# A streaming encoder step on one core: gate products ahead of the position mixing, low parts of the gate weights ahead of the squares, a place of its own for the high part of u

## What is computed

```python
z = h @ w_in + b_in
a = z[..., :2 * D_CONV]
uv = z[..., 2 * D_CONV:2 * D_CONV + 2 * D_GMLP]
gates = jax.nn.sigmoid(z[..., 2 * D_CONV + 2 * D_GMLP:])
a = jax.nn.glu(a, axis=-1)
a = jax.nn.silu(layer_norm(depthwise_causal_conv(a_full, conv_w, conv_b), ln_g, ln_b))
y_a = a @ w_a
uv = jax.nn.gelu(uv)
u, v = uv[..., :D_GMLP], uv[..., D_GMLP:]
v = layer_norm(v, v_ln_g, v_ln_b)
y_b = spatial_gate(u, v, w_s, b_s) @ w_b      # per group of 128 channels: u * (w_s @ v + b_s)
merged = gates[..., :D_MODEL] * y_a + gates[..., D_MODEL:] * y_b
return merged @ w_o, new_hist, v
```

## Time and profile before

| | |
|---|---|
| time before, median of 3 runs | 964.99 us (964.0 to 968.25) |
| span of the profiled execution | 963.2 us |
| TensorE busy | 845.6 us (88%) |
| VectorE busy | 509.0 us (53%) |
| ScalarE busy | 190.9 us (20%) |
| GpSimd busy | 168.8 us (18%) |
| mean granted TensorE clock | 0.940 of full speed |

### The profile page before, as it was taken

One profiled execution on the slowest core, in us unless ns is written; L12 is line 12 of the kernel. 1 busy time (PEld: TensorE's weight loads), 2 busy tenths in 40 slices (PEclk: granted clock), 3 DMA queues, 4 the chain that ended last, 5 costly groups with the idle time before them and its releaser, 6 DMA issues. The chain is left out here.

```text
span 963.2 us, 12133 instructions
## 1 busy us (share of the span) xinstructions
PE 845.6 (88%) x4994; PEld 618.5 (64%) x4994; DVE 509.0 (53%) x753; ACT 190.9 (20%) x284; POOL 168.8 (18%) x156
## 2 busy tenths in 40 slices
PE   2899999999998879979999999917999987979776
PEld 1688886347997879978878644605666655545432
DVE  1328999999999443351365543481333331222236
ACT  3211211111233121741120011201111110101003
POOL 1000000000045454143223000001122221121110
PEclk9899999999998889989999999856999998989899
DMA  9923225011332131365999593242999999999936
GB/s 323 315 64 88 65 67 174 1 44 44 89 88 57 48 88 45 88 219 175 316 314 322 186 381 149 97 193 83 411 404 416 415 418 394 368 406 394 373 110 248
DMA packets 112600, 204.16 MB, mean 212 GB/s; under 512 B 9484, under 2 KB 68212, under 8 KB 104350
## 3 DMA queue, kind: packets, MB, share of 16 engines
q1 hardware_dynamic: 94192, 159.36, 46.5%
q10 hardware_dynamic: 12830, 34.93, 9.6%
q0 software_dynamic: 5520, 9.06, 2.5%
HBM read 199.49 MB, written 14.84 MB: 223 GB/s over the span
## 5 line engine op out<-in xcount | busy, mean ns | idle before, releaser
L858 PE MATMUL PS<-arena 128*64 128x256 f32 (+1 forms) x1056 | 148.7, 411 | 30.2 <-issue 25.7
L1280 DVE SCALAR_TENSOR_TENSOR arena<-arena,VT 128x574 f32<-128x574 f32 x240 | 175.1, 811 | 0.0
L858 PEld LDWEIGHTS PS<-arena 128*64 128x64 f32 (+1 forms) x1056 | 108.8, 156 | 65.4 <-issue 36.9
L1695 POOL TENSOR_TENSOR wL<-arena,wH 128x1024 fp32r<-128x1024 f32 x32 | 83.2, 2621 | 360.8 <-ACT wH L998 360.8
L552 PE MATMUL PS<-arena 128*128 128x272 f32 x512 | 119.1, 396 | 1.6 <-DVE arena L1242 1.6
L552 PEld LDWEIGHTS PS<-arena 128*128 128x128 f32 x512 | 98.3, 192 | 22.1 <-issue 1.6
L619 PE MATMUL PS<-gH,wH 128*128 128x272 f32 x384 | 83.0, 299 | 9.1 <-POOL wL L1695 5.5
L1591 DVE TENSOR_TENSOR arena<-PS,arena 128x256 f32<-128x256 f32 x19 | 8.1, 424 | 140.1 <-ACT arena L1114 140.1
L619 PE MATMUL PS<-gL,wH 128*128 128x272 f32 x384 | 81.9, 296 | 0.0
L619 PE MATMUL PS<-gH,wL 128*128 128x272 f32 x384 | 81.7, 294 | 0.0
L878 PE MATMUL PS<-arena 128*64 128x512 f32 (+1 forms) x264 | 69.1, 597 | 1.4 <-DVE arena L1595 1.4
(11 more groups left out here) (282 smaller groups left out, 996.9 us busy)
## 6 DMA issues: line engine op xcount, KB each, us to landing
arena<-w_gate SPq DMA_DIRECT2D x32, 1024.0 KB, 7.3
arena<-w_up SPq DMA_DIRECT2D x32, 1024.0 KB, 15.4
arena<-w_down ACTq DMA_DIRECT2D x28, 1024.0 KB, 13.9
arena<-w_in SPq DMA_DIRECT2D x40, 512.0 KB, 5.2
arena<-w_ada SPq DMA_DIRECT2D x8, 2048.0 KB, 14.4
vecs<-w_ada SPq DMA_DIRECT2D x4, 2048.0 KB, 9.3
arena<-x_prompt SPq DMA_DIRECT2D x8, 512.0 KB, 8.0
arena<-w_in SPq DMA_DIRECT2D x4, 1024.0 KB, 6.3
```

The costliest lines, as they stand in the source:

```text
L858: last = pe.matmul(PS[h * rows:(h + 1) * rows, 2, n * DE:(n + 1) * DE], hG[:, b, k * SLOTS + h * rows:k * SLOTS + (h + 1) * rows], buf[r / ...
L1280: dve.scalar_tensor_tensor(out=total, in0=src, scalar=tap, in1=total, op0=ALU.mult, op1=ALU.add).then_inc(conv_step, 1)
L1695: pool.tensor_tensor(wL2[q % 2][:, m], WP[q % 2][:, m], wH2[q % 2][:, m], ALU.subtract).then_inc(gw_split, 1)
```

## The change

- TensorE: the order becomes gate 0, histories, gate 1, histories, gate 2, `over_features(6)`, gates 3, 4, 5, then four times two mixes and one gate (gates 6 to 9), gates 10 to 13, `over_features(4)`, gates 14 and 15. The output projection starts when the last but one branch product is merged, and waits for `merged` tile by tile in its first product.
- GpSimd: no gain and bias of v. The low parts of gate unit 2 come ahead of the wait for v, those of units 3, 4 and 5 ahead of the squares.
- VectorE: all of v, in the order of the tiles. The low parts of u (`low_of(0, uT, uL)`) follow the sum of the squares, ahead of the wait for `c_std`.
- ScalarE: the copies of u's high part, four behind the drain of gate 10 and four behind that of gate 12. The root, the first branch unit's high part, the drain of gate 14, swish of tiles 0 to 3, the drain of gate 15, swish of tiles 4 to 7.
- Memory: `yH` and `vecs` share a place behind the arena, `cT32` gets its own, the first buffer of the conditioning weights (`AW[0]`) moves to the place of `gL`, `c16` and `iotaI` lie in the place of u at the start of the program.
- SyncE: the first conditioning weights are loaded when gate 15 is done.

```diff
-        yH, uL, aL = split_parts("yH", O_X, KT, T), split_parts("uL", O_U, KT, T), split_parts("aL", O_C, KT, CONV)
+        yH, uL, aL = split_parts("yH", ARENA, KT, T), split_parts("uL", O_U, KT, T), split_parts("aL", O_C, KT, CONV)
...
-        AW = [vecs[:, 0:KT * BLK].rearrange("p (k n) -> p k n", n=BLK), view(O_S, KT, BLK)]
+        AW = [view(O_X, KT, BLK), view(O_S, KT, BLK)]
...
-            sp.wait_ge(gated, KT)
+            sp.wait_ge(w_used, U_YB)
             load_mod(0)
-            sp.wait_ge(w_used, U_YB)
             load_mod(1)
...
             histories(FULL - HIST)
+            gate(2)
             pe.wait_ge(conv_sum, 1)
             pe.wait_ge(hist_copied, 2)
             over_features(6, rstdc)
-            gate(2)
             gate(3)
+            gate(4)
+            gate(5)
             for h in range(0, KT, 2):
...
                 mix(h + 1)
-                gate(4 + h // 2)
-            for j in range(8, 12):
+                gate(6 + h // 2)
+            for j in range(10, 14):
                 gate(j)
             pe.wait_ge(conv_sum, 2)
             pe.wait_ge(dve_drained, KT)
             over_features(4, rstdc)
-            for j in range(12, NGATE):
-                gate(j)
+            gate(14)
+            gate(15)
...
-            pe.wait_ge(merged, KT)
+            pe.wait_ge(dve_drained, KT + NGATE - 1)
...
                     for k in range(KT):
+                        if (t, hf) == (0, 0):
+                            pe.wait_ge(merged, k + 1)
...
+            gate(8)
+            gate(9)
+            high_gate(6)
+            gate(10)
+            high_u(0)
+            gate(11)
+            high_gate(7)
+            gate(12)
+            high_u(4)
+            gate(13)
             act.wait_ge(stat_ps, 2)
             act.activation(two(rstdc[:, :]), PS[:, 4:6, 0:CH], ACT.Sqrt, bias=eps[:, :]).then_inc(c_std, 1)
...
             high_of(U_YB)
-            gate(NGATE - 2)
-            gate(NGATE - 1)
-            for j in range(EARLY, KT):
-                act.activation(yH[:, j, :], uT[:, j, :], ACT.Copy).then_inc(y_high, 1)
+            gate(14)
+            swish_a(0)
+            gate(15)
+            swish_a(4)
...
             dve.wait_ge(squared, KT)
             add_tiles(sq)
+            low_of(0, uT, uL)
             dve.wait_ge(centred, KT)
             dve.wait_ge(c_std, 1)
...
             low_gate(0)
             low_gate(1)
-            pool.wait_ge(bc_in, 64)
-            for t in (3, 4):
-                vt = v[0:WIDTH[t], t, :]
-                pool.wait_ge(v_scaled, t - 2)
-                pool.tensor_tensor(vt, vt, vgb[0:WIDTH[t], :], ALU.mult).then_inc(v_gained, 1)
-                pool.wait_ge(v_gained, t - 2)
-                pool.tensor_tensor(vt, vt, vbb[0:WIDTH[t], :], ALU.add).then_inc(v_norm, 1)
+            low_gate(2)
             pool.wait_ge(v_norm, TT)
             pool.dma_start(v_out, v[0:NSAMPLE, 4, :]).then_inc(v_stored, 16)
-            low_gate(2)
             low_gate(3)
+            low_gate(4)
+            low_gate(5)
             pool.wait_ge(mix_ps, KT)
...
-            for q in range(4, 16):
+            for q in range(6, 16):
                 low_gate(q)
```

More of the change, by code:

```diff
@@ L104, in build @@
         b3 = halves_of(O_X + KT * T, D)
-        arena = sb("arena", [P, ARENA])
+        with ExitStack() as place:
+            place.enter_context(nc.sbuf_tensor("iota_before", [P, O_U + 2816], F32))
+            iotaI = place.enter_context(nc.sbuf_tensor("iotaI", [P, SLOTS], I32))[:, :]
+        arena = sb("arena", [P, ARENA + KT * T])
         def view(at, *dims):
@@ L178, in build @@
         pick = sb("pick", [P, 2])
-        vecs = sb("vecs", [P, KT * T])
-        cT32 = vecs[:, 4096:KT * T].rearrange("p (k c) -> p k c", c=NSAMPLE)
+        vecs = view(ARENA, KT * T)
+        cT32 = sb("cT32", [P, KT, NSAMPLE])
         bsb = vecs[:, 0:1024].rearrange("p (h t) -> p h t", t=P)
         bvb, vgb, vbb = (vecs[:, 1024 * n:1024 * (n + 1)] for n in (1, 2, 3))
-        h2T = vecs[:, :].rearrange("p (k t) -> p k t", t=T)
-        AW = [vecs[:, 0:KT * BLK].rearrange("p (k n) -> p k n", n=BLK), view(O_S, KT, BLK)]
+        h2T = view(ARENA, KT, T)
+        AW = [view(O_X, KT, BLK), view(O_S, KT, BLK)]
         afb = [vecs[:, D * s:D * (s + 1)] for s in range(2)]
@@ L194, in build @@
         S1 = sb("S1", [P, 2, KT])
-        c16 = sb("c16", [16, P])
+        c16 = view(O_U + 2688, P)[0:16, :]
         brow = sb("brow", [2, 2, BLK])
@@ L1056, in _, with high_u, swish_a @@
             act.wait_ge(hist_ps, 2)
[L1057 to L1060, removed]
+            def high_u(first):
+                act.wait_ge(gated, KT)
+                for j in range(first, first + 4):
+                    act.activation(yH[:, j, :], uT[:, j, :], ACT.Copy).then_inc(y_high, 1)
+            def swish_a(first):
+                for j in range(first, first + 4):
+                    act.wait_ge(c_normed, j + 1)
+                    for at, n, c0 in ((0, NPROMPT, 0), (NPROMPT, NSAMPLE, SAMPLE0)):
+                        act.activation(aT[:, j, at:at + n], cv[:, j, c0:c0 + n], ACT.Silu,
+                                       bias=VT[:, COL_LB + j:COL_LB + j + 1], scale=VT[:, COL_LG + j:COL_LG + j + 1]).then_inc(a_ready, 1)
+            gate(8)
[8 more added lines that the diff above has]
+            gate(13)
             act.wait_ge(stat_ps, 2)
             act.activation(two(rstdc[:, :]), PS[:, 4:6, 0:CH], ACT.Sqrt, bias=eps[:, :]).then_inc(c_std, 1)
[L1063 to L1069, removed]
             high_of(U_YB)
-            gate(NGATE - 2)
-            gate(NGATE - 1)
-            for j in range(EARLY, KT):
-                act.activation(yH[:, j, :], uT[:, j, :], ACT.Copy).then_inc(y_high, 1)
+            gate(14)
+            swish_a(0)
+            gate(15)
+            swish_a(4)
             for n in range(1, 5):
@@ L1311, in _ @@
             then(dve.reciprocal(vsd[:, 0:TT], vsd[:, 0:TT]))
-            for t in (3, 4, 0, 1, 2):
+            for t in range(TT):
                 w = WIDTH[t]
                 vt = v[0:w, t, :]
[L1315 to L1319, removed]
+                then(dve.tensor_scalar(vt, vt, mv[0:w, t, 0:1], vsd[0:w, t:t + 1], ALU.subtract, ALU.mult))
                 then(dve.tensor_tensor(vt, vt, vgb[0:w, :], ALU.mult))
@@ L1340, in _, with low_of @@
                 dve.tensor_tensor(uT[:, h, :], uT[:, h, :], tmp[:, b, 0:T], ALU.mult).then_inc(gated, 1)
+            def low_of(before, src, dst):
+                for j in range(KT):
+                    dve.wait_ge(y_high, before + j + 1)
+                    dve.tensor_tensor(dst[:, j, 0:T], src[:, j, 0:T], yH[:, j, :], ALU.subtract).then_inc(y_split, 1)
             dve.wait_ge(squared, KT)
             add_tiles(sq)
+            low_of(0, uT, uL)
             dve.wait_ge(centred, KT)
@@ L1348, in _ @@
                 dve.tensor_tensor(cv[:, j, :], cv[:, j, :], rstdc[:, :], ALU.mult).then_inc(c_normed, 1)
[L1351 to L1354, removed]
             def merge(j):
@@ L1383, in add_bias @@
                 ins.then_inc(mod_added, 1)
[L1385 to L1392, removed]
             dve.wait_ge(gate_drained, NGATE)
```

8 lines of the change are left out of this document (3 added, 5 removed).

## The result

| | before | changed |
|---|---|---|
| time, median | 964.5 us (4 runs, 962.95 to 968.25) | 939.34 us (4 runs, 938.02 to 940.93) |
| ratio, 95% interval | | 0.9724 (0.9694 to 0.9753) |
| span of the profiled execution | 963.2 us | 939.1 us |
| TensorE busy | 845.6 us | 837.4 us |
| mean granted TensorE clock | 0.940 | 0.949 |

The change is faster by 25.2 us, 2.8%. The forecast was 937.3 us with a range of 932 to 946.

The account below looks back on a forecast made before the run. TensorE, busy 88% of the span, bounds the kernel. Gains of 26.0 us at the gates and 1.7 us at the projection, 27.7 us in all, take the span from 963.2 to 935.5; median 1.8 above: 937.3 us, range 932 to 946.

Parts of the forecast that it names:

- The bound and the stretch: TensorE from the end of the second histories to the first merged branch product: 137.3 us before, 111.3 forecast.
- To the first mix: Gates 2 to 5 cover v and its centring; v ready at 313.7, centring done at 319.1, TensorE waits 0.4 us.
- The squares and the gates: Squares start when the mixes end, their sum ends between 361.7 and 376.2; the 5.5 us wait for weights goes.
- The end of the gates: TensorE, through its gates at 390.8, idles 4.0 us until ScalarE has drained gate 15 at 394.8.
- The half clock behind the wait: TensorE at half clock after the wait ahead of the first branch product: 2.2 us lost, 1.5 to 2.8.
- The table loads: ScalarE's three switches at the end of the gates: 1.28 us each; by the skill page 4.1 us more, forecast 941.
- The projection: Output projection: the 1.7 us wait for the last merge goes; 0.9 us gain if the weight load is a us late.
- 1 (cover lost): Gates lose their cover somewhere; waits of 3 to 6 us at two places give back 8 to 16: 945 to 953; chance 0.10.
- 2 (the experts take it back): The weight-bound expert stage takes the gain back, little but the projection's wait counts: 960 to 965 us; chance 0.06.
- 3 (VectorE and GpSimd block each other): GpSimd's low parts and squares each hold up a VectorE instruction by 2.1 us: slower, 983 us; chance 0.04.
- 4 (u waits for something else): u's high part waits for something besides its place; 4 us and half clock stay: 941 to 944, within the forecast's 0.80.
- the last wait: TensorE's wait for ScalarE's drains ahead of the first branch product: 4.0 us, replacing 4.1 us for u's parts.

Follow-up runs that it names:

- second profile: The changed kernel timed and profiled once more, with no edit, against the kernel before: median 937.98 us, ratio 0.9704.

## Why the prediction was right

**The bound and the stretch.** 104.7 us of work in the stretch was taken from a gate, a pair of mixes and an average; the kernels that never fall to half clock show 104.35. The forecast of 111.3 us came out at 110.7.

**To the first mix.** v was to be ready 21.0 us after VectorE began it and took 20.4 (294.7 to 315.1): two instructions met GpSimd's, at 2.1 us each, against 4.7 allowed. TensorE waited 0.3 us where 0.4 was forecast. That this order is what pays is shown by the kernel with the old one, 13 to 14 us slower.

**The squares and the gates.** The squares started as the mixes ended and no gate waited for weights. Putting one unit behind them cost 8.8 us. Their sum took 0.8 + 8.9 us, between the bounds, and ended at 368.1, ten us before it was due.

**The end of the gates.** Right in place and mechanism, with two sizes off that cancel, which is luck. The wait was 4.5 us, 4.0 forecast. Of the difference, 0.24 us is a swish of 4.39 instead of 4.15 us: VectorE's second and third normalised tile took 2.94 us each beside GpSimd, so the third came at 392.24. Another 0.21 us lies between the end of the drain (396.43) and TensorE's start (396.64), which the forecast had put at nothing. The half clock behind the wait cost 1.5 us instead of 2.2, and other profiles show up to 2.5 for the same wait.

**The table loads.** Three switches lie on this path, and the drain of gate 15 ends 9.7 us after the first of their loads begins (386.69 to 396.43): 3 x 1.28 us of loads and 5.8 us of activations leave 0.1 us for anything else. The Trainium skill (ScalarE: Activation LUTs, "What ACT_TABLE_LOAD costs") gives 2.66 us for a switch; the trace shows 1.28, and the measurement decides.

**The projection** was mis-sized: 1.7 us forecast, 1.0 had, since the second half of `w_o` landed 0.7 us late. The forecast had called it "just in time" and put the gain at 0.9 us if the load were a us late. The 1.0 us is read from the traces; the timings do not settle it.

**The rest.** From the first merge to the end the profiles take 534.1 us before, 534.6 in the changed kernel and 532.0 in its second profile, and between 530.9 and 535.5 over all kernels, so this part scatters by more than the start does. The span of 939.1 lies 3.6 us above the 935.5 forecast: 2.0 more at the start, 0.6 less in the stretch, and 2.2 more behind the first merge, 0.7 of it for `w_o`. The second profile has 936.2.

**The rivals.** 1 (cover lost): no such wait. 2 (the experts take it back): the stretch is shorter by 26.6 us, and the span by 24.1 in the first profile and 27.0 in the second. 3 (VectorE and GpSimd block each other): with gain and bias of two tiles on GpSimd, VectorE has less to do and is still busy 4.5 us longer, and the time does not move. 4 (u waits for something else): in the changed kernel no such wait is there. In the old order the waits for u's parts went and waits for drains came in their place; alone, the own place gives 1.5 us or nothing, and in the changed kernel it saves 1.2 us of wait. My prediction let the last wait take "the place of 4.1 us for u's parts", which is what happened. The end of the gates still gave 6 of the 26.6 us, because more than those 4.1 us stood there. The rows of before, two waits and one of the two windows at half clock:

```profile
PE PS L619 <- ACT arena L1040: 1.8, 1, 1.8
...
PE PS L619 <- DVE uL L1354: 1.5, 1, 1.5
```

```profile
407.30:410.70 3.40, 3.40 (x17) 3.40 (x16) 0.00 (x0) 3.39 (x8) 0.00 (x0) 0.51 0.00 0
```

With the 4.1 us and the 6.2 us window, three waits (7.4 us in all) and two parts at half clock (some 4.8 us lost) cost 12 us before; one wait and one such part cost 6.0 now.

## What to carry to other kernels

Follow an in-order queue for what stands in front of the instruction that the bounding engine waits for, not only for what that instruction needs: the largest thing left here was a drain of 0.7 us behind 5.7 us of table load and swish that TensorE did not need yet, and moving one line gave 5 us. Removing the last wait in a chain shows only what the one before it hid: u's own place alone gave nothing that can be told in the old order, and taking it out of the new one brought 1.2 us of wait. Independent products are best spent ahead of the long chain on other engines, and the engine that prepares their operands must get the same order.

## What the runs showed of the hardware

Idle time of 3.7 us and more was followed by time at half clock in the stretch of every profile here. Measured as busy time above 104.35 us: a 4.5 us wait was followed by a part at half clock (0.51 granted) that cost 1.5 us, a 5.7 us wait by 2.6, and the same 4.5 us wait behind another of 5.6 brought the two to 5.4. Waits of 1.0 us cost nothing behind them (granted clock 1.00 in the kernels that drain gate 15 first). In the kernel before a wait of 1.8 us was followed by 3.4 us at half clock (from 407.3, granted 0.51), and waits of 1.5 and 1.7 us were not (granted 1.00 from 427.2 to 433.0 and from 547.3 to 553.0). In one profile the same 4.5 us cost 2.5, with the same instructions in the stretch, so the price varies between executions by a microsecond.

A tensor_scalar on one SBUF tensor was held up by GpSimd as the two-input instructions were (2.89 us against 0.81), while the centring, with one operand in PSUM, took 0.67 us a tile whether GpSimd was busy beside it or not (5.37 us for eight in the changed kernel, with GpSimd at work from 316.2 us, and 5.37 us with TensorE's old order, where GpSimd computed nothing between 303.0 and 318.0).
